# Second block of a two-block transformer kernel: its attentions by halves of the heads, with products and modulation slabs between the quads

## What is computed

```python
h = x * (1.0 + sc_t) + sh_t
# layer 0: _dsa_mixer (16 heads of 64, top-k of an index score picks 64 keys); layer 1: _diff_mixer
y = mixer(h)
x = _layer_norm(DN_ALPHA * x + (1.0 + g_t) * y, ln_g[i, 0], ln_b[i, 0])
h = x * (1.0 + sc_c) + sh_c
y = jnp.square(jax.nn.relu(h @ w1)) @ w2
x = _layer_norm(DN_ALPHA * x + (1.0 + g_c) * y, ln_g[i, 1], ln_b[i, 1])
...
# _diff_mixer: 8 heads of two softmaxes each, their difference times v, and a norm for each head
p = jax.nn.softmax(logits, axis=-1)
a = p[:, :, 0] - lam_full * p[:, :, 1]
o = jnp.einsum('bhqs,bshe->bqhe', a, v)
o = _rms_norm(o, subln_g) * (1.0 - lam_init)
return o.reshape(B, S, B_HEADS * 2 * B_HEAD_DIM) @ w_o
```

## Time and profile before

| | us |
|---|---|
| three runs: lowest, median, highest | 1277.41, 1280.69, 1281.82 |
| the profiled execution | 1289.1 |
| its span | 1287.4 |
| mean granted clock of TensorE | 0.931 |

### The profile page before, as it was taken

The page is one execution under the profiler, slowest core; times in us unless marked ns, Lnnn a source line. Parts: engine busy times, 40 slices in busy tenths (PEclk is TensorE's granted clock), DMA queues, the critical chain, the costliest instruction groups (busy, mean ns, idle before and its releaser), DMA issues.

```text
span 1287.4 us, 16290 instructions
## 1 busy us (share of the span) xinstructions
PE 1140.8 (89%) x6742; PEld 963.6 (75%) x6742; DVE 505.7 (39%) x689; ACT 550.4 (43%) x761; POOL 767.6 (60%) x373
## 2 busy tenths in 40 slices
PE   5898988897989889799789999999799569999995
PEld 5787867686868766587677888797777358998994
DVE  4556452337665333216636301106400655401014
ACT  4554563345454632344433444343333433544441
POOL 5676654656857556272015877887356115988883
PEclk9899998998989889999579999999899669999998
DMA  5754533455535335856003766675588204565640
GB/s 206 245 168 160 196 109 120 147 201 207 201 128 196 99 115 156 306 169 195 26 6 125 278 248 243 229 245 180 197 310 295 99 0 131 195 196 165 197 164 33
DMA packets 101023, 221.60 MB, mean 172 GB/s; under 512 B 11360, under 2 KB 17878, under 8 KB 94806
## 3 DMA queue, kind: packets, MB, share of 16 engines
q1 hardware_dynamic: 95776, 210.29, 48.0%
q10 hardware_dynamic: 5174, 10.28, 2.3%
HBM read 219.48 MB, written 1.07 MB: 171 GB/s over the span
## 4 chain that ended last, share of the span: by engine, by line
PE 66%; DVE 12%; DMA 7%; ACT 6%; POOL 4%; issue 4%; ACTq 0%; SPq 0%; POOLq 0%; DVEq 0%
PE lin_ps L337 12%; PE lin_ps L338 11%; PE lin_ps L339 11%; PE tmp_ps L344 4%; PE tmp_ps L346 4%; PE tmp_ps L345 4%; POOL wlo L847 4%; PE tmp_ps L399 3%; PE tmp_ps L548 3%; PE tmp_ps L449 2%; PE lin_ps L344 2%; ACT whi L947 2%; PE lin_ps L346 2%; PE lin_ps L345 2%; DMA ring<-in_w_in 2%
## 5 line engine op out<-in xcount | busy, mean ns | idle before, releaser
L847 POOL TENSOR_TENSOR wlo<-ring,whi 128x1024 fp32r<-128x1024 f32 (+2 forms) x304 | 735.2, 2431 | 430.4 <-ACT whi L947 427.8
L947 ACT CAST whi<-ring 128x1024 fp32r<-128x1024 f32 (+2 forms) x304 | 312.9, 1034 | 513.9 <-PE lin_ps L339 257.2
L337 PE MATMUL lin_ps<-whi,hThi 128*128 128x512 f32 (+2 forms) x528 | 213.7, 405 | 28.9 <-POOL wlo L847 11.0
L338 PE MATMUL lin_ps<-wlo,hThi 128*128 128x512 f32 (+2 forms) x528 | 207.5, 393 | 0.0
L339 PE MATMUL lin_ps<-whi,hTlo 128*128 128x512 f32 (+2 forms) x528 | 207.0, 392 | 0.0
L337 PEld LDWEIGHTS lin_ps<-whi,hThi 128*128 128x128 f32 x528 | 104.2, 197 | 61.5 <-issue 20.8
L344 PE MATMUL tmp_ps<-hThi,whi 128*128 128x256 f32 x520 | 147.8, 284 | 2.1 <-DVE hTlo L1583 1.2
L346 PE MATMUL tmp_ps<-hThi,wlo 128*128 128x256 f32 x520 | 147.2, 283 | 0.0
L345 PE MATMUL tmp_ps<-hTlo,whi 128*128 128x256 f32 x520 | 147.2, 283 | 0.0
L344 PE MATMUL lin_ps<-hThi,whi 128*128 128x256 f32 x352 | 103.5, 294 | 21.1 <-POOL wlo L847 17.8
L339 PEld LDWEIGHTS lin_ps<-whi,hTlo 128*128 128x128 f32 x528 | 103.8, 197 | 20.7
(11 more groups left out here) (250 smaller groups left out, 1581.5 us busy)
## 6 DMA issues: line engine op xcount, KB each, us to landing
ring<-in_mlp_w SPq DMA_DIRECT2D x64, 1024.0 KB, 5.3
ring<-in_ada_w SPq DMA_DIRECT2D x48, 1024.0 KB, 5.8
ring<-in_w_in SPq DMA_DIRECT2D x40, 1024.0 KB, 5.3
ring<-in_b_w_in SPq DMA_DIRECT2D x12, 1024.0 KB, 5.7
ring<-in_w_out SPq DMA_DIRECT2D x8, 1024.0 KB, 5.1
ring<-in_a_w_in SPq DMA_DIRECT2D x6, 1024.0 KB, 9.2
ring<-in_w_up_hgrn SPq DMA_DIRECT2D x4, 1024.0 KB, 5.1
ring<-in_w_up_attn SPq DMA_DIRECT2D x4, 1024.0 KB, 5.1
```

The lines of the kernel that those rows point to most:

```text
L337: pe.matmul(ps, xh, hi, start=first, stop=False, skip_group_check=True)
L338: pe.matmul(ps, xh, lo, start=False, stop=False, skip_group_check=True)
L847: pool.tensor_tensor(wlo[:, n % PARTS, :, 0:width], ring[:, u % RING, 2 * h:2 * h + 2, 0:width], whi[:, n % PARTS, :, 0:width].bitcast(F32 ...
L947: act.copy(whi[:, n % PARTS, :, 0:width], ring[:, u % RING, 2 * h:2 * h + 2, 0:width]).then_inc(S("high_formed"), 1)
```

## The change

It has four parts.

1. **Halves of the heads.** The quads of both attentions of the second block go (i, g) = (0,0), (0,1), (1,0), (1,1), then the same with g = 2, 3. So the first half of `lin_ps` holds the output of the first eight (in `s2` four) heads for all tokens, and it is scaled, normed and turned (`output_turned(name, 0)`) ahead of the last product.
2. **The projection** goes y0 with the first four k tiles, then the second half's transposes, then y1 with the first four, y0 and y1 with the last four.
3. **`s2`:** only q0, k0 and v0 are made first. q1, k1 and v1 are fills of the first four quads, with two slabs behind the second's scores, four behind the fifth quad and two behind the sixth. ScalarE's copies of q1, k1, v1 stand between its exponentials.
4. **Slabs:** two more visits of two slabs in `s1`'s MLP (groups 1 and 6) in place of two in `s2`; in `s0` the first visit stands behind the product `s0iq`, not ahead of it.

A wait of the first block's VectorE for the second output half, which ends with the first now, is gone as well. The line numbers after are some 30 higher on all engines but TensorE.

```diff
-ADA_FILLED = (2, 3, 4, 5)
+ADA_FILLED = (1, 2, 3, 4, 5, 6)
...
-                    if n == 0:
-                        product.ps = open_lin(f"{name}o0", half)
-                    if g == 0 and i == 1 and ocols == D:
-                        product.ps = open_lin(f"{name}o1", 1 - half)
+                    part = g // 2
+                    if n in (0, 4):
+                        product.ps = open_lin(f"{name}o{part}", half ^ part)
...
+                    if n in after:
+                        after[n]()
...
+            def output_turned(name, part):
+
+                wait_read(f"{name}o{part}")
+                transposes(f"{name}oT{part}", [hs[:, i, k * P:(k + 1) * P]
+                                               for k in range(4 * part, 4 * part + 4) for i in range(NT)])
+                operand_ready(*turned(f"{name}oT{part}", 4 * part))
+
             def project(name, w):
-                feature_major(f"{name}oT", hs)
-                operand_ready(*turned(f"{name}oT0", 0), *turned(f"{name}oT1", 4))
-                for c in range(2):
-                    linear_tok(f"{name}y{c}", w, c * HALF, HALF, hT)
+
+                def part(c, k0):
+                    linear_part(f"{name}y{c}", w, c * HALF, HALF, hT, k0, half=turn_lin[f"{name}o{c}"][0])
+
+                ada_close()
+                part(0, 0)
+                output_turned(name, 1)
+                part(1, 0)
+                part(0, 4)
+                part(1, 4)
...
-            quads_16 = [(i, g) for i in range(NT) for g in range(4)]
+            quads_16 = [(i, 2 * part + g) for part in range(2) for i in range(NT) for g in range(2)]
...
+            linear_feat("s0iq", w, 1280, hT)
             ada(2)
-            linear_feat("s0iq", w, 1280, hT)
...
+                      {9: [lambda half: output_turned("s0", 0)]})
...
-            for n in range(2):
-                for part in range(2):
-                    linear_feat(f"s2{'qk'[part]}{n}", w, part * D + n * HALF, hT)
-                    ada(2)
-            for n in range(2):
-                linear_tok(f"s2v{n}", w, 2 * D + n * HALF, HALF, hT)
-                ada(2)
+            linear_feat("s2q0", w, 0, hT)
+            linear_feat("s2k0", w, D, hT)
+            linear_tok("s2v0", w, 2 * D, HALF, hT)
             ada_close()
-            wait_read(*(f"s2{part}{n}" for part in "qkv" for n in range(2)))
+            wait_read("s2q0", "s2k0")
+
+            def queries(half):
+                feat_units("s2q1", open_lin("s2q1", half), w, HALF, hT)
+
+            def keys(half):
+                feat_units("s2k1", open_lin("s2k1", half), w, D + HALF, hT)
+
+            def values(k0):
+                return lambda half: linear_part("s2v1", w, 2 * D + HALF, HALF, hT, k0, half=half)
+
+            def landed(*names):
+                return lambda half: wait_read(*names)
+
+            def slabs_between(n):
+                return lambda half: ada(n)
+
             attention("s2", quads_16, heads(qT), heads(kT),
-                      lambda b, head: vv[:, b, head * P:(head + 1) * P], P, 2, D, (Pq_second, pT_second), lag=2)
-            wait_read("s2o0", "s2o1")
+                      lambda b, head: vv[:, b, head * P:(head + 1) * P], P, 2, (Pq_second, pT_second),
+                      {0: [queries], 1: [slabs_between(2), keys], 2: [values(0), landed("s2v0")],
+                       3: [values(4), landed("s2q1", "s2k1")],
+                       6: [landed("s2v1")], 10: [lambda half: output_turned("s2", 0)]}, lag=2,
+                      after={4: lambda: ada(4), 5: lambda: ada(2)})
...
+            projected("q", 0)
+            projected("k", 0)
+            norm_weights(2)
+            gate_bias(1, 1)
+            projected("v", 0)
+            attention("s2", quads, 2, (Pq_second, pT_second),
+                      evacuate={1: lambda: projected("q", 1), 2: lambda: projected("k", 1),
+                                4: lambda: projected("v", 1), 7: lambda: heads_norm(0)}, lag=2)
...
+            low_of("s0oT0", 0)
             scaled_out(1)
-            for h in range(2):
-                low_of(f"s0oT{h}", 4 * h)
+            low_of("s0oT1", 4)
...
-            for _ in range(6):
-                ada()
...
+                if n in (1, 4, 5):
+                    ada()
+            heads_variance(0)
             combine(7)
-            for i in range(NT):
-                heads_variance(i)
-                heads_scaled(i)
-            for h in range(2):
-                low_of(f"s2oT{h}", 4 * h, lams[:, 4:5])
+            heads_scaled(0)
+            low_of("s2oT0", 0, lams[:, 4:5])
+            heads_variance(1)
+            heads_scaled(1)
+            ada_close()
+            low_of("s2oT1", 4, lams[:, 4:5])
...
```

More of the change, by code:

```diff
@@ L452, in ada, with attention @@
                 finished(name, event)
-            def attention(name, quads, q, k, v, vw, per, ocols, bufs, fills=None, lag=1, half=None):
+            def attention(name, quads, q, k, v, vw, per, bufs, fills=None, lag=1, half=None,
+                          after={}):
                 def scores(n):
@@ L856, in rstd @@
                 pool.wait_ge(S(f"{name}var"), 1)
-                power = half[:, :, 0] if len(v.shape) == 2 and v.shape[1] == NT else half[:, 0, :] if len(v.shape) == 2 else half[:]
+                power = half[:, :, 0] if len(v.shape) == 2 else half[:, :, 0:v.shape[2]]
                 pool.tensor_tensor(y, v, power, ALU.pow).then_inc(S(f"{name}rstd"), 1)
@@ L893, in _ @@
             rstd("s1ln", mv[:, :, 1], one, "s1y1")
-            for i in range(NT):
-                rstd(f"s2h{i}", st[:, 1, i, :], st[:, 2, i, :], f"s2o{i}")
+            for part in range(2):
+                cols = slice(4 * part, 4 * part + 4)
+                rstd(f"s2h{part}", st[:, 1, :, cols], st[:, 2, :, cols], f"s2o{part}")
             rstd("s2ln", mv[:, :, 1], one, "s2y1")
@@ L1190, in _ @@
                 read(act.copy(flat(kT[:, 4 * h:4 * h + 4, :]), flat(ps)), f"s0k{h}")
-            quads = [(i, g) for i in range(NT) for g in range(4)]
+            quads = [(i, 2 * part + g) for part in range(2) for i in range(NT) for g in range(2)]
             attention("s0", quads, QUAD, (Pq_second, pT_second))
@@ L1197, in _, with projected, heads_norm @@
             mixed("s2", 1, 0)
[L1198 to L1213, removed]
+            def projected(part, n):
+                ps = full_lin(f"s2{part}{n}")
+                if part == "v":
+                    ins = act.copy(vv[:, :, n * HALF:(n + 1) * HALF], ps)
+                else:
+                    dst, scale = (qT, HD ** -0.5) if part == "q" else (kT, 1.0)
+                    ins = act.mul(flat(dst[:, 4 * n:4 * n + 4, :]), flat(ps), scale)
+                read(ins, f"s2{part}{n}")
+            def heads_norm(part):
+                ps = full_lin(f"s2o{part}")
+                act.activation(osq[:, :, part * HALF:(part + 1) * HALF], ps, ACT.Square).then_inc(S("s2osq"), 1)
+            projected("q", 0)
[6 more added lines that the diff above has]
+                                4: lambda: projected("v", 1), 7: lambda: heads_norm(0)}, lag=2)
+            high_of("s2oT0", 0, lams[:, 4:5])
             heads_norm(1)
-            for h in range(2):
-                high_of(f"s2oT{h}", 4 * h, lams[:, 4:5])
+            high_of("s2oT1", 4, lams[:, 4:5])
             ahead("s2y1")
@@ L1528, in _ @@
                 dve.wait_ge(S(f"{name}prob"), 4)
-                dve.wait_ge(*done[f"{name}o1"])
                 ps = full_lin_of(dve, f"{name}o0")
@@ L1716, in total_s0, with scaled_out @@
                                ).then_inc(S("s0prob"), 1)
[L1718 to L1723, removed]
+            def scaled_out(part):
+                dve.wait_ge(S("s0prob"), 4 * part + 4)
+                ps = full_lin_of(dve, f"s0o{part}")
+                for i in range(NT):
+                    ins = dve.tensor_tensor(hs[:, i, part * HALF:(part + 1) * HALF].rearrange("p (h d) -> p h d", h=8),
+                                            ps[:, i, :].rearrange("p (h d) -> p h d", h=8),
+                                            rden[:, i, 8 * part:8 * part + 8].unsqueeze(2).broadcast_to([P, 8, HD]),
+                                            ALU.mult)
+                read(ins, f"s0o{part}")
             for n, (i, g) in enumerate(quads):
```

39 lines of the change are left out of this document (20 added, 19 removed).

## The result

The changed kernel takes 1267.3 us (median of 4 runs, 1261.8 to 1268.3) against 1281.3 of the kernel before: a ratio of 0.987 (95% interval 0.983 to 0.991). It is faster by 14 us, not by the 33 of the forecast, and lies above the range.

What follows compares the result with a forecast made beforehand. One stage was taken to starve on DMA and the next on softmax. 7.7 + 0 - 0.5 - 3.7 + 29.5 - 0.5 = 32.5 us takes the profiled 1289.1 to 1256.6 and the median 1280.7 to 1248; range 1236 to 1262 (8 in 10).

Steps and rivals of the forecast that it cites:

- s0iq: Product ahead of s0's attention: with the two slabs behind it, it starts earlier; gain 7.7 us, 3.8 to 10.0.
- `s0`'s attention: Second block's first attention, by halves: saved idle and transposes offset a slower projection start; 0, within 3 us either way.
- The residual's 0.5: Behind the projections of s0 and s2: VectorE finishes later because both column halves end close together; loss 0.5 us each.
- Slabs in `s1`: Two more visits of two slabs in s1's MLP, where TensorE is never idle; loss 3.7 us, upper bound 6.
- s2: From its first product to the end of its projection: 172.7 us becomes 143.2, gain 29.5.
- fills: In s2, q1, k1 and v1 made between the first four quads' scores, with their softmax free beside them; 42.7 us.
- open part: In s2, behind the fills up to the projection, including a 14.9 us wait for slabs and b_w_o; 37.7 us.
- hops: In s2's sum, an allowance for some fifteen hops of 0.1 us; 1.5 us.
- (a): Rival: q1, k1 and v1's two parts each start at the lower clock, 9.8 us more, 1258; chance 0.20.
- (b): Rival: landings are hidden, so the sixth quad's exponentials in s2 are ready some 9 us earlier, 1239; chance 0.12.
- (c): Rival: ScalarE serialises fills and softmax, the first four quads' chain is uncovered, some 14.5 us return, 1262; chance 0.06.
- (d): Rival on the slower side, with fills and projection at a low clock; chance 0.04.

Runs made afterwards that it cites:

- iq_back: The changed kernel with the two slabs ahead of the product s0iq again; 1275.0 us, ratio 0.994 to the kernel before.
- turn_first: The changed kernel with the transposes of quad n-2 ahead of the fill behind quad n's scores, in s2 alone; 1253.5 us, ratio 0.975 to the kernel before.
- cast_late: The changed kernel with ScalarE's three casts of b_w_o behind the copy of the sixth quad's probabilities; 1263.5 us, ratio 0.981 to the kernel before.
- before_again: The kernel before, unchanged, for a second profiled execution; 1284.1 us, ratio 0.999 to its group's other runs of this kernel.
- both: The changed kernel with the edits of turn_first and cast_late together; 1250.0 us, ratio 0.972 to the kernel before.
- cast_last: The kernel of both, with b_w_o's casts behind the last copy of probabilities and POOL's first head-norm root ahead of their low parts; 1245.2 us, ratio 0.970 to the kernel before.

## Why the prediction was wrong

By its own steps:

1. **`s0iq`: right in the mechanism, and 7.7 in part by luck.** The product started at 537.84 (forecast 538.0), ended at 549.81 (550.5), and the index scores came at 553.84 (555.1). At the index scores 9.2 us were gained (from `s0`'s first product 33.6 before, 24.4 after), 1.5 more than forecast. Then the next product started at the lower clock (granted 0.59 in its first 2.6 us) and took 13.26 us where it took 11.77 before, which I had not forecast, so that up to the attention it was 7.7 again. In the second execution that product ran at a granted clock of 1.00, and the gain was 9.5. `iq_back` shows that the gain is this order's.
2. **`s0`'s attention: once beyond its bounds.** 0, within 3, was forecast. 3.9 and 1.2 were gained; no run takes the cause apart. The eight profiled executions with halves have 76.4 to 79.6 for this piece, the two without have 80.3 and 80.5. The residual's 0.5 was 0.2 or none here and 0.3 behind `s2`.
3. **Slabs in `s1`: 4.3 for 3.7.** Each of the two visits takes 1.85 us from start to start, and a few tenths come on top.
4. **`s2`: wrong by 13.9.** The pieces, forecast and measured: until the first scores 36.2 and 35.6; fills 42.7 and 50.5; open part 37.7 and 48.2; projection 25.1 and 22.8; hops 1.5 and, inside the pieces, none.

The prediction had said when it would be wrong: with fills over 45 us, or a stretch behind them far from 37.7. Both came.

The step that failed is the sentence "The softmax of the first four quads (at most 1.4 + 1.2 + 2.0 + 2.0 = 6.6 us each) lies beside it: free." It compared durations, and did not ask what starts the softmax. The first two masks start at once; the third and fourth wait for transposes that stand behind a fill. This costs 7.8 us in the fills and 3.3 in the open part (the fourth quad's chain, which I had covered). `turn_first` takes that cause away alone, and `s2` falls by 13.1, more than these 11.1: the four slabs run at the higher clock again (granted 1.00 for 0.75; 3.64 us for 4.83), and the tail is 1.0 shorter. Its fills take 42.8 us, and 42.7 was forecast. So the price of the fills was right, for a kernel that has the transposes in front of them.

The second step that failed is the tail of the open part. From the end of the third cast (1006.0) on, 19.8 us were forecast and 26.8 measured. The sum had the sixth quad's exponentials and then one mask and maximum. In fact the seventh quad's scores wait for the copy behind those exponentials, so that two whole quads follow in series, and a large one's scores (2.08), mask and maximum (2.6) and exponentials (2.0) had been left out. `cast_late` confirms who holds the seventh quad: with the casts behind it, the wait of 7.89 is gone.

Two errors went the other way. The projection did not start cold: its first 24 matmuls ran at a granted clock of 1.00 and took 5.73 us where 5.5 + 2.0 were forecast. And the hops of 1.5 were already in the pieces.

Of the rivals, (a) (fills start cold) did not occur: q1 and k1 took 11.78 and 11.76 us each. Only the last quarter of v1, behind its wait of 2.86, ran mostly at the lower clock (granted 0.62): 4.4 us (977.62 to 982.06) where a quarter of 11.1 is 2.8. (b) did not occur, the landing came when forecast. (c) had the result (1262, the first chain not covered, a cast behind exponentials) but gave another cause, and too small a chance (0.06). (d), the slower side (0.04), with fills and projection at a low clock, did not occur: the granted clock was 0.97 through the fills and 1.00 through the projection.

**The sum against the median.** The profiled execution was forecast at 1256.6 and took 1267.25, 10.7 more: 13.9 in `s2`, less 3.9 in `s0`, and 0.7 in the rest. The other 8.6 of the 19.3 us by which the forecast of the median missed are not in these pieces. I had set the gain of 32.5 against the median of the kernel before, which lies 8.4 below its profile. The changed kernel's profile lies at its own median, and `before_again` has 1.8 (1285.84 for 1284.06) where the first profile had 8.4, so one execution's distance from a median is no constant. But by the medians themselves the change gains only 14 and 16 us where its pieces have 22, so 6 to 8 us would have been missed from any median. If the pieces behind the first block are as long in the timed executions as in the profiled one (an estimate, nothing shows it), the first block took 521 to 524 us there in the kernel before and 525 to 530 in the eight runs with the change, while the profiles have 525.3 and 529.2 against 523.7 to 530.5. Whether the change costs time in the first block stays open. The range had no room for any of this.

## What to carry to other kernels

Before work is called covered by a fill, list what starts each step of it, and look where the releaser stands in the filled engine's program: a buffer that is reused after n steps makes the fill a link of the chain that it should hide. Work that serves the chain (here a transpose of 0.4 us) goes ahead of the fill, and prefetching steps that can wait for DMA go behind the last step of the chain that others wait for. And a range for a median needs width for what the pieces of one profile do not tell: here pieces and medians of the same two kernels differ by 6 to 8 us in the gain.

## What the runs showed of the hardware

Some operations of VectorE took much longer beside POOL's low parts. In `both` a VectorE operation of 0.23 us took 2.41, and two that take 0.62 took 4.73, both ending within 0.15 us of a low part of POOL; in `cast_last`, without low parts at that time, they took 0.23 and 0.62. The changed kernel shows it too, at the second quad, with 2.13 us for an operation that takes 0.17 with POOL idle (1013.54):

```profile
948.77 2.13 DVE L1356 TENSOR_SCALAR qst<-qst 128x4 f32<-128x4 f32 x1
...
948.49 2.39 POOL L875 TENSOR_TENSOR wlo<-ring,whi 128x1024 fp32r<-128x1024 f32 x1 [1.19 <-ACT whi L976]
```

In these places VectorE's operations, on 2 and 4 elements of a partition too, took 2.13 to 2.41 us each (4.73 for two) and ended within 0.15 us of a low part's end; a low part takes 2.4 us (4.75 for two). In `both` the two starts are 0.03 us apart, so there the trace does not tell who came first. No run takes the cause apart. Not every operation took longer: in `cast_last`, while POOL formed low parts (1009.62 to 1016.66), an operation with one input in PSUM and a reduction kept the times that they have in the changed kernel with POOL idle (1.41 for two, 1.22), and a `TENSOR_SCALAR` on 8 elements took 1.45 in place of 0.17:

```profile
1012.21 1.41 DVE L1288 SCALAR_TENSOR_TENSOR hTlo<-tmp_ps,lams,hThi 128x512 fp32r<-128x512 f32 x2 [4.21 <-ACT hThi L1006]
1013.97 1.22 DVE L1808 TENSOR_REDUCE st<-arena 128x8 f32<-128x1024 f32 x1 [0.35 <-ACT arena L1246]
1015.23 1.45 DVE L1810 TENSOR_SCALAR st<-st 128x8 f32<-128x8 f32 x1
```

POOL's low parts came out longer too. In the changed kernel's projection the residual's addition, of `x` and `hs`, stands beside them: it took 3.34 us where it takes 1.23 at the end of the kernel with POOL idle, and the two low parts that came next took 5.39 in place of the 4.75 that two take alone (939.75):

```profile
1051.71 3.34 DVE L1640 SCALAR_TENSOR_TENSOR x<-x,hs 128x1024 f32<-128x1024 f32 x1
...
1054.29 5.39 POOL L875 TENSOR_TENSOR wlo<-ring,whi 128x1024 fp32r<-128x1024 f32 x2 [0.32 <-ACT whi L976]
...
1245.36 1.23 DVE L1640 SCALAR_TENSOR_TENSOR x<-x,hs 128x1024 f32<-128x1024 f32 x1
```
